# A layer's steps woven between expert picks: other step sizes and choice places, SyncE spreading the picks, states one a step, step sizes taken in the first norm

## The chip, the cores and the metric

The kernel is one program on one core of a Trainium2 chip. The metric is device time in microseconds (us), the median of several runs. PE is TensorE, DVE is VectorE, ACT is ScalarE, POOL is GpSimd, SP is SyncE. All data are 32-bit floats.

## The reference, cut to what matters

Two layers run over 640 tokens: one prompt of 512 tokens and eight streams of 16 tokens. Each layer has two halves:

```
h  = rmsnorm(x, ln1) * (1 + sc1) + sh1            # sh, sc, g come from silu(c) @ w_mod
z, xbc, dt, lx, ly, g_ssd, g_lru = split(h @ w_in)
dt = softplus(dt + bias)                          # the step size of the SSD scan, 16 heads
y_ssd = rmsnorm(ssd_scan(silu(conv(xbc)), dt, states) * silu(z)) @ w_br_ssd
y_lru = (rglru(conv(lx)) * gelu(ly)) @ w_br_lru
x += g1 * ((sigmoid(g_ssd) * y_ssd + sigmoid(g_lru) * y_lru) @ w_out)

h = rmsnorm(x, ln2) * (1 + sc2) + sh2             # the second norm
q = h @ wq                                        # 8 heads, two half keys each
i1, i2 = top16(q1 @ k1.T), top16(q2 @ k2.T)       # 128 keys each
e, g = top16 of the 256 sums, softmax             # 16 experts a head, 128 a token
x += g2 * sum_k gelu(h . u[e_k]) * g_k * v[e_k]   # "picks": rows u, v of 16384 experts
```

The outputs are the normed x, the new scan states of prompt and streams, and the last rows that the convolutions keep.

## The kernel before, in words

**Tiles and regions.** The 640 tokens are five tiles of 128 (the fifth holds the eight streams). The dense work of a layer is done in two regions: tiles 0 to 2 (384 columns) and tiles 3 and 4 (256 columns). That makes regions 0 to 3 over the two layers, and expert tiles 0 to 9. A region is a list of steps, numbered by `bases`: N1 (first norm, 12 steps), X (10 projections with the short convolution), S (the scan: six or so steps a tile), Z, LX, LRU, M (32 projections for the merge), OUT (8 projections, with the second norm's squares and sums among them; the norm itself, from its ninth step on, has no projection), Q (16 projections and the choice of the experts, 22 steps with the last four having no projection). A projection reads one 512 KB tile of weights, which SP loads into one of four slots (`wslot`) as soon as the projection four before it is done. Region 1 and region 3 also carry the stream states: 32 loads of 256 KB in both together, by SP into five slots, and 16 stores by ACT.

**Picks.** A unit is one pick for each of the 128 tokens: POOL gathers 128 rows of 8 KB (u and v of an expert, 1 MB in all) into a ring of eight slots. DVE takes the dot product with h (`dots`), ACT makes gelu, gate and a small diagonal matrix (`diagonals`), PE multiplies with the v half (`values`) and so frees the slot (`used`). Two units are a pair. A tile has 64 pairs, and there are 640 pairs.

**The order of the work.** `plan` writes one list of (pair, steps) entries that every engine follows in program order. `window` deals a region's steps over a given row of pairs by the weights in `SHARE`: region 1 over what is left of tile 0 and tiles 1 and 2, region 2 over tiles 3 and 4 (pairs 9 to 122), region 3 over tiles 5 to 7 (pairs 9 to 180), the final norm over tiles 8 and 9. PE multiplies the pair before it, then does the steps; DVE takes the pair first, then the steps; ACT does the first step, the pair, then the other steps. Region 0 comes before all pairs but the last few steps.

**The choice.** In Q, DVE finds the best keys of all tiles of the region and completes the choice of the region's first tile. The choice of the other tiles (`sum_up`, `look_up`, `put`, 24 pieces in 24 pairs, then the gates) is made beside the pairs of the tile before: from pair `choice_at(s)` on, which is 24 in tile 0 and 8 in the others. Picks and gates then stand by token and have to be turned to units: `spread` does it with 16 small DMAs, issued by ACT at pair `choice_at(s) + 28`, and for a region's first tile at Q's last step (in region 0 in two halves, at Q 13 and 21). The first gather of a tile waits for its spread.

**dt.** `x_stage` of PE does the dt projection at X's first step, ahead of the first X projection: 8 matmuls of 16 columns for each tile, after the last slice of h.

**States.** `stream_parts` in S of regions 1 and 3, from its step 9 on: two states a step, each a matmul on PE, a multiplication and an addition on DVE, and a store by ACT. SP has all 16 state loads of a layer in one row between the loads for Z 3 and Z 4, and the last three of them wait for stores.

Of the kernel before, what the change touches and what calls it, by code (L numbers as in the profile page):

```python
# [34 lines left out]
SLOTS = 4  # L35
# [22 lines left out]
def bases(g):  # L58
# [8 lines left out]
    b["END"] = b["Q"] + 22  # L67
    return b
# [11 lines left out]
SHARE = {"N1": 4, "X": 14, "S": 10, "Z": 18, "LX": 17, "LRU": 25, "M": 17, "OUT": 10, "Q": 24}  # L80
# [83 lines left out]


# [25 lines left out]
def choice_at(s):  # L191

    return 8 if s else 24
# [38 lines left out]
def build(nc, a):  # L232
    ctx = ExitStack()
    with ctx:
# [164 lines left out]
        with nc.Block() as block:  # L399
            @block.sync  # L400
            def _(sp):
# [31 lines left out]
                def states(l):  # L433

                    lay = G[1]
                    for i in range(16):
# [10 lines left out]
                for r in range(REGIONS):  # L447
                    l, g = divmod(r, 2)
                    if g == 0:
                        small_ones(l)  # L450
                    for j in range(10):
                        load(tile(l, TX + j))
                        if r == 0 and j == 3:
                            for c in range(4, 8):
                                mod_chunk(c)
                        if r == 0 and 4 <= j < 8:
                            mod_chunk(4 + j)
                    if r == 0:
                        for c in range(12, 16):
                            mod_chunk(c)  # L460
                    for j in range(8):
                        if g and j == 4:
                            states(l)
                        load(tile(l, TZ + j))
                        if r == 0 and j >= 4:
                            mod_chunk(12 + j)
                    for j in range(8):
                        load(tile(l, TLX + j))
                        if r == 0 and j < 4:
                            mod_chunk(20 + j)  # L470
                    for j in range(8):
                        load(tile(l, TLY + j))
                        load(a["w_gate"].rearrange("l k p c -> p (l k) c")[:, l * KT + j, :], 2 * P)
                    for j in range(8):
                        for first in (TGS, TBS, TGL, TBL):
                            load(tile(l, first + j))
                    for j in range(8):
                        load(tile(l, TOUT + j))
                    for j in range(16):
                        load(tile(l, TWQ + j))  # L480
# [1492 lines left out]
```

## Time and profile before

| | |
|---|---|
| median of 3 runs | 4614.37 us (4608.49 to 4616.39) |
| profiled execution | 4609.44 us |
| its span, first to last instruction | 4607.7 us |
| PE, DVE busy | 3212.4 us (70%), 2825.9 us (61%) |
| ACT, POOL busy | 1466.3 us (32%), 1436.5 us (31%) |
| DMA | 1610.83 MB, mean 350 GB/s |
| first gather | at 709.0 us |
| last gather | at 4572.5 us |

Busy time is what an engine spent in instructions; the share is of the span. The gathers are 1342 of the 1611 MB. The page divides the span into 40 slices of 115 us; one digit or number of a row is one slice.

### The profile page before, as it was taken

To read this page: it belongs to the slowest core of one execution; us is meant where nothing else is said; L and a number is where in the kernel's file an instruction comes from. 1 tells how busy PE (TensorE), PEld (TensorE's weight loads), DVE (VectorE), ACT (ScalarE), POOL (GpSimd) and SP (SyncE) were. 2 spreads that over 40 slices of the span, in tenths; PEclk is the share of its full clock that TensorE was granted. 3 is DMA by queue.
4 is the path that set the end of the run, shared out by engine and by line. 5 is a ranking of instruction groups with operands and counts; after the bars stand their busy time and mean duration, and the time that the engine had idled before them with its cause. 6 is when DMAs were issued, how large, how long until landed. Compare 5 with 4: busy or idle time off the path is not lost. (4 is left out here: it accounts for less than half of the span.)

```text
span 4607.7 us, 60395 instructions
## 1 busy us (share of the span) xinstructions
PE 3212.4 (70%) x21986; PEld 1895.2 (41%) x21986; DVE 2825.9 (61%) x6591; ACT 1466.3 (32%) x4657; POOL 1436.5 (31%) x1298
## 2 busy tenths in 40 slices
PE   7899994777777664488999864767777664444443
PEld 4455552445454442254555431445555442121111
DVE  2422058695864587676743696965854587675454
ACT  2224012443622222333722222433622222232222
POOL 0000003333334334323333323334334334344332
PEclk8999996878888776589999875778888786555555
DMA  7333328899999999968999978999999999999998
GB/s 320 142 147 101 101 82 320 343 356 379 417 417 419 419 400 396 413 265 311 382 380 378 366 292 364 395 364 406 418 418 419 420 404 390 421 420 421 421 422 336
DMA packets 279860, 1610.83 MB, mean 350 GB/s; under 512 B 56410, under 2 KB 61328, under 8 KB 112524
## 3 DMA queue, kind: packets, MB, share of 16 engines
q0 software_dynamic: 184320, 1342.26, 71.6%
q1 hardware_dynamic: 65808, 255.49, 14.5%
q10 hardware_dynamic: 29436, 9.24, 0.8%
q8 instruction: 174, 2.85, 0.2%
q14 instruction: 122, 1.00, 0.1%
HBM read 1597.63 MB, written 7.91 MB: 348 GB/s over the span
## 5 line engine op out<-in xcount | busy, mean ns | idle before, releaser
L528 POOL DMA_INDIRECT ring<-in_peer_uv,units x1280 | 1433.3, 1120 | 3136.3 <-PE psum L923 2219.9
L1827 DVE SCALAR_TENSOR_TENSOR ring<-ring,hrow 128x1024 f32<-128x1024 f32 x1280 | 1538.4, 1222 | 890.7 <-DMA ring<-in_peer_uv,units 864.3
L923 PE MATMUL psum<-ring,diag 128*32 128x256 f32 x10240 | 926.0, 495 | 1182.9 <-ACT diag L1292 1181.9
L541 PE MATMUL psum<-hT,wslot 128*128 128x384 f32 (+1 forms) x4224 | 1283.0, 461 | 27.7 <-DMA wslot<-in_w_tiles 24.6
L541 PEld LDWEIGHTS psum<-hT,wslot 128*128 128x128 f32 x4224 | 845.7, 205 | 456.9 <-issue 111.1
L923 PEld LDWEIGHTS psum<-ring,diag 128*32 128x32 f32 x10240 | 322.2, 131 | 1705.1 <-ACT diag L1292 1394.1
L1282 ACT ACTIVATE gel<-hid 128x2 f32<-128x2 f32 x640 | 129.1, 202 | 1935.5 <-DVE ring L1827 1881.0
L541 PE MATMUL psum<-region,wslot 128*128 128x384 f32 (+1 forms) x1536 | 446.8, 446 | 5.5 <-DVE xT L1682 2.2
L541 PEld LDWEIGHTS psum<-region,wslot 128*128 128x128 f32 x1536 | 293.8, 195 | 152.0 <-issue 28.2
L1292 ACT ACTIVATE diag<-pick,wgt 128x32 f32<-128x32 f32 x1280 | 331.7, 306 | 0.0
L1286 ACT ACTIVATE wgt<-gel,units 128x1 f32<-128x1 f32 x1280 | 307.4, 287 | 20.9
L1449 DVE SCALAR_TENSOR_TENSOR region<-region,vec 128x384 f32<-128x384 f32 (+1 forms) x144 | 80.8, 561 | 145.6 <-ACT region L1056 142.4
L945 PE MATMUL psum<-ident,hT 128*32 128x128 f32 x2816 | 129.6, 343 | 37.8 <-ACT hrow L1322 28.4
L945 PEld LDWEIGHTS psum<-ident,hT 128*32 128x32 f32 x2816 | 108.7, 143 | 71.7 <-issue 26.9
L1194 ACT ACTIVATE region<-psum 128x384 f32<-128x384 f32 (+1 forms) x64 | 27.6, 431 | 315.3 <-PE psum L541 305.3
L1827 DVE DVE_READ_ACCUMULATOR ring<-ring,hrow 128x1 f32 x1280 | 104.1, 81 | 0.0
L1662 DVE SCALAR_TENSOR_TENSOR region<-region,psum 128x384 f32<-128x384 f32 (+1 forms) x32 | 15.5, 485 | 142.7 <-PE psum L541 142.6
L1586 DVE SCALAR_TENSOR_TENSOR region<-region,psum 128x384 f32<-128x384 f32 (+1 forms) x32 | 15.5, 485 | 117.8 <-ACT region L1138 117.8
L1656 DVE SCALAR_TENSOR_TENSOR region<-region,psum 128x384 f32<-128x384 f32 (+1 forms) x32 | 15.5, 485 | 110.8 <-PE psum L541 67.1
L1282 ACT ACT_TABLE_LOAD x60 | 77.0, 1283 | 13.1 <-issue 10.9
L572 PE MATMUL psum<-ring,cT 128*32 128x512 f32 x384 | 47.9, 618 | 30.9 <-DMA ring<-in_w_modt 15.6
L1017 ACT ACTIVATE region<-psum 128x512 f32<-128x512 f32 x24 | 14.3, 597 | 153.6 <-PE psum L580 141.8
(247 smaller groups left out, 2806.0 us busy)
## 6 DMA issues: line engine op xcount, KB each, us to landing
wslot<-in_w_tiles SPq DMA_DIRECT2D x360, 512.0 KB, 7.7
ring<-in_w_modt SPq DMA_DIRECT2D x24, 2048.0 KB, 9.0
ring<-in_peer_uv,units POOLq DMA_INDIRECT x1280, 13.7
wslot<-in_w_gate SPq DMA_DIRECT2D x32, 128.0 KB, 9.6
region<-in_states_t SPq DMA_DIRECT2D x16, 256.0 KB, 13.2
region<-in_states_n SPq DMA_DIRECT2D x16, 256.0 KB, 10.0
out_new_ssd_sample<-region ACTq DMA_DIRECT2D x16, 256.0 KB, 15.4
xT<-in_x_t SPq DMA_DIRECT2D x1, 2560.0 KB, 8.9
```

What stands on the lines that cost most here:

```text
L528: pool.indirect_dma_start(ring[:, n, :], None, table, bass.IndirectOffsetOnAxis(ap=units[:, s % 2, block, 0, quad:quad + 1].bitcast(U32), ...
L541: last = pe.matmul(out, wslot[:, n % SLOTS, k * P:(k + 1) * P], src(k), start=k == 0, stop=k == KT - 1)
L572: last = pe.matmul(bank(5)[32 * q:32 * q + 32, :], cT[:, 2 * q + kk, :], w, start=kk == 0, stop=kk == 1)
L923: last = pe.matmul(psum[c * BLOCK:(c + 1) * BLOCK, block % 2, block // 2 * 256:(block // 2 + 1) * 256], diag[:, n, :], ring[:, n, D + c * ...
L945: last = pe.matmul(out[c * BLOCK:(c + 1) * BLOCK, :], v, ident[:], start=True, stop=True)
L1194: act.activation(lay.gates[:, q, :], bank(3 + 2 * q)[:, 0:lay.N], ACT.Tanh, scale=0.5).then_inc(S["mg"], 1)
L1282: act.activation(gel[:, v], hid[:, v], ACT.Gelu_apprx_tanh).then_inc(E["gelu"], 1)
L1286: act.activation(wgt[:, c:c + 1], gel[:, c:c + 1], ACT.Copy, scale=units[:, s % 2, block, 1, quad + u:quad + u + 1])\
L1292: act.activation(diag[:, pick % RING, :], pick32[:], ACT.Copy, scale=wgt[:, pick % 16:pick % 16 + 1])\
L1449: st(dve.scalar_tensor_tensor(y, x[:, k:k + NY], w(k), y, ALU.mult, ALU.add))
L1586: st(dve.scalar_tensor_tensor(lay.zt, lay.zth[:, j % 2, :], 1.0, bank(3 + j % 2)[:, 0:lay.N], ALU.add, ALU.mult))
L1827: dve.scalar_tensor_tensor(out=ring[:, n, 0:D], in0=ring[:, n, 0:D], scalar=1.0, in1=hrow[:, e % 2, :], op0=ALU.mult, op1=ALU.mult, accum_ ...
```

## The change

Five things change. (1) `SHARE` has two more entries: the norm part of OUT (`N2`) and Q's last four steps (`QE`) get small sizes of their own, OUT's projections a larger one, and S and LRU move by one. (2) The choice beside tiles 0 and 3 starts at pair 30, not 24 and 8. (3) SP issues the spreads instead of ACT, between its weight loads, in the order of the plan. (4) The dt matmuls are dealt over steps 6 to 9 of N1 as the slices of h come; the stream tile's stay at X 0. (5) States go one a step in eight steps, not two a step in four; the last three state loads of a layer stand behind the loads for LX 0, 1 and 2.

```diff
+    b["N2"], b["QE"] = b["OUT"] + 9, b["Q"] + 18
-SHARE = {"N1": 4, "X": 14, "S": 10, "Z": 18, "LX": 17, "LRU": 25, "M": 17, "OUT": 10, "Q": 24}
+SHARE = {"N1": 4, "X": 14, "S": 11, "Z": 18, "LX": 17, "LRU": 24, "M": 17, "OUT": 18, "N2": 3, "Q": 24, "QE": 6}
...
 def choice_at(s):
-    return 8 if s else 24
+    return {0: 30, 3: 30}.get(s, 8)
...
# SP: the loads become a generator, weights(), and the plan is walked
-                        if g and j == 4:
-                            states(l)
+                            if g and j == 4:
+                                states(l, range(13))
...
+                            yield load(tile(l, TLX + j))
+                            if g and j < 3:
+                                states(l, (13 + j,))
...
+                def spread(s, h):
+                    sp.wait_ge(E["ready"], s + h + 1 if s == 0 else s + 2)
+                    if s >= 2:
+                        sp.wait_ge(E["wgt"], (s - 1) * UNITS)
+                    c = slice(h * length(s), (h + 1) * length(s)) if s == 0 else slice(0, QUADS)
+                    for block in range(BLOCKS):
+                        for r in range(BLOCKS):
+                            sp.dma_start(units[...], picked[...]).then_inc(E["spread"], 16)
+                ahead, taken = weights(), 0
+                for e, steps in PLAN:
+                    while n < min(taken + SLOTS, REGIONS * LOADS):
+                        next(ahead)
+                    if e and e[0] < TILES_E and same_group(e[0]) and e[1] == choice_at(e[0]) + 28:
+                        spread(e[0] + 1, 0)
+                    for r, i in steps:
+                        if r < REGIONS:
+                            taken += loads_in(r, i)
+                            if r == 0 and i == BASE[0]["Q"] + 13:
+                                spread(0, 0)
+                            if i == BASE[r]["Q"] + 21:
+                                spread(TILE0[r], passes(TILE0[r]) - 1)
...
# PE, x_stage
+                def steps_of_dt(lay, u, k):
+                    return pe.matmul(bank(7)[:, u * HEADS:(u + 1) * HEADS], hT[:, k, lay.t0 + u * P:lay.t0 + (u + 1) * P],
+                                     wdt[:, k * HEADS:(k + 1) * HEADS], start=k == 0 and u == 0, stop=k == KT - 1, skip_group_check=True)
+                    if -6 <= i < -2:
+                        if i == -6:
+                            pe.wait_ge(S["mean"], at("mean", 2 * r))
+                            pe.wait_ge(loaded["wdt"], 16 * (l + 1))
+                        pe.wait_ge(S["modulated"], at("modulated", 2 * r, 2 * i + 13))
+                        for k in (2 * i + 12, 2 * i + 13):
+                            for u in range(lay.nt - lay.sample):
+                                last = steps_of_dt(lay, u, k)
...
# PE, stream_parts; DVE and ACT alike
-                    if 9 <= i <= 12:
+                    if 9 <= i <= 16:
+                        j = i - 9
-                        for j in (2 * i - 18, 2 * i - 17):
...
# ACT: spread() and its three calls are gone
-                    if r == 0 and i == 13:
-                        spread(0, 0)
-                    if i == 21:
-                        spread(s, passes(s) - 1)
...
-                        if p == choice_at(s) + 28:
-                            spread(s + 1, 0)
```

## Rows read from the trace of the kernel before

**Rows 1.** The page: the span, and GB/s moved in 40 slices.

```profile
span 4607.7 us, 60395 instructions
GB/s 320 142 147 101 101 82 320 343 356 379 417 417 419 419 400 396 413 265 311 382 380 378 366 292 364 395 364 406 418 418 419 420 404 390 421 420 421 421 422 336
```

**Rows 2.** Busy time in stretches (length, engines, PEclk, DMA, GB/s): regions 1, 2, 3; tile 9.

```profile
817.00:1932.00 1115.00, 747.84 (x6035) 486.70 (x6028) 765.00 (x1776) 389.98 (x1335) 420.99 (x371) 0.79 0.98 396
1932.00:2861.00 929.00, 762.99 (x4548) 416.21 (x4546) 613.59 (x1451) 326.26 (x942) 296.10 (x256) 0.88 0.88 342
2861.00:3995.00 1134.00, 759.88 (x5992) 490.20 (x5984) 784.50 (x1808) 396.31 (x1368) 438.72 (x387) 0.79 1.00 405
...
4260.00:4540.00 280.00, 120.61 (x1120) 47.65 (x1120) 143.63 (x242) 70.73 (x296) 108.86 (x112) 0.54 1.01 421
```

**Rows 3.** The page's DMA issues: count, KB each, median us to landing.

```profile
wslot<-in_w_tiles SPq DMA_DIRECT2D x360, 512.0 KB, 7.7
...
ring<-in_peer_uv,units POOLq DMA_INDIRECT x1280, 13.7
...
region<-in_states_t SPq DMA_DIRECT2D x16, 256.0 KB, 13.2
```

**Rows 4.** The spreads: line L1303; timeline about tile 5's; SP's loads.

```profile
L1303 ACTq DMA_DIRECT2D units<-picked x176: 513/612/1439, 696.5 to 4139.0; - x176
...
2780.66 9.74 ACTq L1303 DMA_DIRECT2D units<-picked  x15
...
2792.82 0.94 POOL L528 DMA_INDIRECT ring<-in_peer_uv,units  x1 [7.41 <-PE psum L923]
...
L408 SPq DMA_DIRECT2D wslot<-in_w_tiles x360: 327/328/4229, 6.9 to 3774.4; - x180
```

**Rows 5.** Timeline of PE and POOL (start, us, instruction, idle before): dt of region 0; a gather.

```profile
46.16 10.43 PE L594 MATMUL psum<-wdt,hT 128*128 128x16 f32 x48 [9.30 <-ACT hT L1008]
...
1975.62 0.94 POOL L528 DMA_INDIRECT ring<-in_peer_uv,units  x1 [26.86 <-PE psum L923]
```

**Rows 6.** States: SP's timeline in region 1, and waits of the whole span.

```profile
996.91 57.48 SPq L444 DMA_DIRECT2D region<-in_states_n  x8
...
DVE region L1567 <- DMA region<-in_states_n: 30.7, 4, 12.7
...
PE psum L541 <- DMA wslot<-in_w_tiles: 24.6, 2, 13.2
```

**Rows 7.** Stretches of region 2: X, S, LX, LRU, OUT, N2, Q, QE; last, region 3's N1.

```profile
1955.00:2039.00 84.00, 77.17 (x368) 45.72 (x368) 61.03 (x142) 31.57 (x92) 21.86 (x19) 0.87 0.71 271
2039.00:2126.00 87.00, 65.53 (x523) 35.55 (x523) 81.02 (x141) 38.49 (x85) 23.82 (x18) 0.81 0.65 244
...
2179.00:2236.00 57.00, 55.77 (x344) 30.58 (x344) 41.97 (x72) 24.14 (x74) 17.88 (x16) 1.00 0.92 345
2236.00:2299.00 63.00, 61.38 (x304) 33.32 (x305) 46.93 (x88) 57.34 (x106) 22.53 (x21) 1.00 1.02 414
...
2507.00:2557.00 50.00, 50.00 (x234) 28.36 (x234) 16.70 (x31) 9.68 (x33) 10.01 (x10) 1.00 0.78 298
2557.00:2578.00 21.00, 10.24 (x119) 4.23 (x117) 18.43 (x32) 13.32 (x34) 11.55 (x10) 0.72 0.97 377
2578.00:2750.00 172.00, 133.30 (x788) 75.97 (x788) 145.81 (x542) 42.47 (x144) 50.41 (x47) 0.86 0.89 343
2750.00:2781.00 31.00, 8.22 (x88) 3.78 (x92) 29.03 (x96) 7.23 (x23) 6.58 (x6) 0.50 0.55 206
...
2861.00:2886.00 25.00, 12.93 (x120) 6.58 (x112) 24.35 (x51) 13.51 (x39) 10.93 (x9) 0.70 1.01 420
```

**Rows 8.** Region 2, DVE on the choice's tile `both` alone, in N1, X and S.

```profile
1932.00:1955.00 23.00, 6.78 (x15) 0.71 1.00 404
1955.00:2039.00 84.00, 12.05 (x33) 0.87 0.71 271
2039.00:2126.00 87.00, 16.25 (x40) 0.81 0.65 244
```

More of the change, by code:

```diff
@@ L163, with loads_in @@
 POS = weight_positions()
+LOADS = 98
+TILE0 = [NT * (r // 2) + FIRST[r % 2] for r in range(REGIONS)]
+def loads_in(r, i):
+    return sum(each for name, count, each in (("X", 10, 1), ("Z", 8, 1), ("LX", 8, 1), ("LRU", 8, 2), ("M", 32, 1), ("OUT", 8, 1), ("Q", 16, 1))
+               if 0 <= i - BASE[r][name] < count)
 PER = {"zeroed": 2, "sampled": 2, "modset": 3, "zscaled": 8, "xfill": 18, "conved": 18, "tapped": 18, "kept": 18, "xth": 10, "silued": 10, "acb": 2, "ea": 2, "seg": 4, "e": 4, "w": 2, "y": 2, "ys": 2,
@@ L431, in small_ones, with states @@
                     sp.dma_start(kT[:], a["keys"].rearrange("p (l i k) -> p l i k", l=DEPTH, i=2)[:, l, :, :]).then_inc(loaded["keys"], 16)
-                def states(l):
+                def states(l, loads):
                     lay = G[1]
-                    for i in range(16):
+                    for i in loads:
                         slot = i % 5
@@ new lines, in spread @@
+                def spread(s, h):
[5 more added lines that the diff above has]
+                        for r in range(BLOCKS):
+                            sp.dma_start(units[r * BLOCK:(r + 1) * BLOCK, s % 2, block, :, c],
+                                         picked[block * BLOCK:(block + 1) * BLOCK, s % 2, r, :, c]).then_inc(E["spread"], 16)
@@ L482, in _ @@
+                for _ in ahead:
+                    pass
             @block.gpsimd
@@ L585, in x_stage @@
                     lay = G[g]
+                    if -6 <= i < -2:
[6 more added lines that the diff above has]
+                                last = steps_of_dt(lay, u, k)
+                        if i == -3 and not lay.sample:
+                            last.then_inc(S["dt_mm"], 1)
                     if i == 0:
@@ L589, in x_stage @@
                             pe.wait_ge(S["sampled"], at("sampled", l, 0))
-                        pe.wait_ge(S["mean"], at("mean", 2 * r))
-                        pe.wait_ge(loaded["wdt"], 16 * (l + 1))
-                        for u in range(lay.nt):
                             for k in range(KT):
-                                last = pe.matmul(bank(7)[:, u * HEADS:(u + 1) * HEADS],
-                                                 hT[:, k, lay.t0 + u * P:lay.t0 + (u + 1) * P],
-                                                 wdt[:, k * HEADS:(k + 1) * HEADS], start=k == 0, stop=k == KT - 1)
-                        last.then_inc(S["dt_mm"], 1)
+                                last = steps_of_dt(lay, lay.nt - 1, k)
+                            last.then_inc(S["dt_mm"], 1)
                     if 0 <= i < 10:
@@ L1293, in diagonals @@
                            .then_inc(E["diag"], 1)
-                def spread(s, h):
-                    act.wait_ge(E["ready"], s + h + 1 if s == 0 else s + 2)
-                    if s >= 2:
-                        act.wait_ge(E["wgt"], (s - 1) * UNITS)
-                    c = slice(h * length(s), (h + 1) * length(s)) if s == 0 else slice(0, QUADS)
-                    for block in range(BLOCKS):
-                        for r in range(BLOCKS):
-                            act.dma_start(units[r * BLOCK:(r + 1) * BLOCK, s % 2, block, :, c],
-                                          picked[block * BLOCK:(block + 1) * BLOCK, s % 2, r, :, c]).then_inc(E["spread"], 16)
                 def take_out(o):
```

100 lines of the change are left out of this document (50 added, 50 removed).

## The prediction

> **What bounds the kernel now.** I read the page's slices first, for where the DMA engines are not full, then the busy time of each stretch between the regions' borders, then the waits and landings, and last the timeline at the places where POOL stood longest.
>
> From the seventh slice on the kernel moves gathers, and where nothing else holds it, it moves 417 to 422 GB/s [rows 1]. In tile 9 alone 112 gathers take 280 us, 2.50 us each, at 421 GB/s [rows 2]: a pair costs 5.0 us of DMA and a 512 KB weight tile 1.25 us (0.524 MB over 418 GB/s). Bytes are fixed, so what can be won after the first gather is the time in which the rate is under 418. A stretch loses its length times (1 - rate/418): region 1, 1115 x (1 - 396/418) = 59 us; region 2, 929 x (1 - 342/418) = 169 us; region 3, 1134 x (1 - 405/418) = 35 us [rows 2]. That is 263 us, two thirds of it in region 2, which has 384 columns in every projection and only 113 pairs to hide them. POOL's waits name PE's values, as in [rows 5], but that is only the ring coming free: it says "ring full" in a stretch at 418 GB/s and "late consumers" in one at 300, so I don't price by them.
>
> Within region 2 [rows 7]: X loses 84 x (1 - 271/418) = 30 us (PE 77 of 84 busy at clock 0.87); S loses 36 us (DVE 81 of 87); LX 10; LRU 1; OUT 14 (PE 50 of 50); Q 31 (DVE 146 of 172); QE 16 (DVE 29 of 31). So the path alternates: PE in X, Z to M and OUT, DVE in S, Q and QE.
>
> **The change part by part.** The sum is made against the profiled execution, 4609.4 us, which is 5 us under the median of the three runs.
>
> *dt in the norm's steps.* Region 0 has 24 dt matmuls (48 instructions with the weight loads) in 10.4 us, 0.434 us each, after PE has waited 9.3 us for the last slice of h [rows 5]; region 2 has as many and the same pattern, X 0 stands behind them, and POOL's wait there, 26.9 us, is the longest [rows 5]. Dealt over the slices, two slices are 6 matmuls, 2.6 us. Region 0: the slices come every 0.6 us and the dt work takes 1.3 us a slice, so it starts with the second slice, some 3.5 us before the last: 3.5 us off the serial part ahead of all gathers. Region 2: six slices are out 5 us before the last two there, because a pair and a choice piece stand between, so 7.8 of the 10.4 us go into the wait: 7 us. In regions 1 and 3 one tile of two moves, 8 matmuls = 3.5 us each; these are nearer to DMA-bound, so 4 us for both. Against it: PE now waits in steps 6 to 9 for what ACT does two steps later, with its next values queued behind, so a ring slot may come free a pair's length (5 us) late in three regions; the cover is the ring. I take 15 us, bounds 0 and 28 (10.4 twice and 3.5 twice).
>
> *Spreads from ACT to SP.* 176 issues at 0.612 us hold ACT at each of the 11 spreads, 9.74 us for 15 issues, 10.3 with the first [rows 4]; ACT's diagonals, which PE's values and then the ring wait for, are behind. About tile 5's spread POOL stood 7.4 us [rows 4]. The ring holds four pairs, 20 us of DMA, of which 13.7 are a gather's flight [rows 3], so about 6 us of a 10.3 us block are covered and 4 us are lost where DMA is the bound. The first spread has no pair behind it and gains nothing; tile 5's comes at the last moment (pair 57 of 61) and its gather waits for the landing wherever it is issued, so half of it stays. Ten spreads at up to 4.3 us are 43; tiles 2, 3, 7 and 9 have theirs in full-rate stretches where the row of slices shows no dip [rows 1], so I count six at 3 us: 17 us, bounds 0 and 35. On SP each issue costs between 0.328 us, a weight load's, and ACT's 0.612 [rows 4]: 5 to 10 us in which no weight is loaded, with four tiles loaded ahead, which PE takes in over 20 us (a projection with 384 columns is 5 us, and there is a pair between). No wait of PE, then, beyond the two priced next. A wait is added to SP: the spread waits for the choice, and what stands behind it is the next weight load and, in region 3, the states.
>
> The Trainium skill ("DMA: Bandwidth & Descriptors", section "Issuing engines are not separate DMA queues") says that issuing from another engine saves only the sequencer's issue time, usually small against the transfer. Here the issue time is 10.3 us a spread and the transfer 8 KB, so the row speaks against it; by the rule as written the 17 us would go and the median be 4581 (three quarters of 44), inside the forecast's own range.
>
> *States one a step.* SP sat in the second eight state loads for 57.5 us, and Z 4's weights stood behind [rows 6]: PE waited 24.6 us in all for weights, twice, both there, and DVE 30.7 us for states [rows 6]. With the last three loads put behind LX 0 to 2 and the others not waiting for stores, the 24.6 go; the DVE waits shrink, since a step has one state where it had two. They overlap, and Z's stretches are near DMA-bound, so the 24.6 and 30.7 are worth less than their sum: 19 us for both regions. Against it, in region 3 the spread for tile 6 (pair 36) now stands on SP ahead of the states, where before they were loaded right after Z 3's weights; PE wants the first at pair 38, two pairs or 13 us after the choice is ready, and they come after 5 to 10 us of issues and a landing of 13 [rows 3]: 5 us late, up to 10. I take 14 us, bounds 0 and 30.
>
> *Choice from pair 30.* Beside tile 3 the choice lay wholly in N1, X and S: 6.8, 12.1 and 16.3 us of DVE [rows 8]. Pairs 30 to 53 are S's last two, Z, LX and most of LRU. S was DVE-bound: 81 - 16 + 3 = 68 us of DVE against PE's 66, so 87 becomes about 75: 12 us. N1's chain runs on DVE with the 6.8 us of pieces between: 4 us. X is PE-bound: 4 us. Given back: LX had DVE 42 of 57 and gets 12, LRU 47 of 63 and gets 9 [rows 7], both then almost as full as PE: 3 and 4 us. Net 13 us, bounds -15 (all 35 us reappear, less what S gives) and 30. Beside tile 0 it moves six pairs and I take 2 us. What is late next: the gates are ready at pair 57 and the spread must land before the first gather of the next tile, at pair 61. That is three pairs and more, 18 us in region 1 and 21 in region 2, against 5 to 10 of issues and a landing of 13.7 at most, if it is as slow as a gather's. It fits narrowly; if not, 0 to 5 us each.
>
> *Step sizes.* Worked out from `window`: region 2's S goes from 10 pairs to 11, Z from 7 to 8, OUT from 5 to 8, N2 from 5 to 2, Q and QE together from 27 to 24, M from 29 to 30. OUT and N2 keep 10 pairs together and their time is PE's eight projections plus the norm's chain (50 + 21 us [rows 7]) however they are dealt. Three pairs leave a DVE-bound stretch (3 x 2.4 us) and go where they cost 1.5 to 2.4 each. In regions 1 and 3, N2 gets nine steps in three pairs; region 3's N1 already does twelve in four at 420 GB/s [rows 7], so nothing is lost there. QE's four steps in two pairs put 14 to 17 us of DVE between two dots, against about 14 us of cover: 3 us lost in each region, about what the pairs moved out of Q win. I take 0, bounds -15 and 20.
>
> *Sum.* 15 + 17 + 14 + 13 + 2 + 0 = 61 us. Several of these claim the same lost time (in region 2's first stretches dt and choice, in region 1's Z spread, states and clock), and a stretch that is freed from one holder meets the next; I take three quarters, 46. Then 4609.4 - 46 = 4563, and 4568 for the median.
>
> **The rivals.**
>
> *SP becomes the holder (slower).* If a spread keeps SP from weights for longer than the four slots last, PE stands in M, LX and Q of the regions. Place: the spreads for tiles 1, 2, 4, 6 and 7, and the first loads of regions 1 to 3. It decides from the point where the wait for the choice plus the issues plus a weight's landing (0 + 10 + 8 us) pass four projections with their pairs (25 us). For it: SP is in order, and DVE may be two steps behind PE, which makes the 0 into 10. Against: PE cannot run on without DVE's reads of its banks. Price: 10.3 us of block plus a 2 us late landing at each of eight places, 98 us, against the other parts without the spread's gain (44 x 3/4 = 33): 4609 + 65 = 4674, 4679 as a median.
>
> *Spread queued behind weights.* Spread and weights now share SP's queue. The weights' landing is 7.7 us [rows 3], so a spread issued just behind one lands as much later, and that falls on the first gather of tiles 1, 4 and 5, where there is no slack: 3 x 8 = 24 us. Time 4563 + 24 = 4587, 4592 as a median. For it: tile 5's was tight before; against: when its spread is due the weights of region 3 landed long ago. The Trainium skill (same page, section "Queues, rings and completion order") says that on each DMA engine a queue's descriptors are taken in order while the engine goes round between queues, which is this mechanism.
>
> *Given back.* The ring hides the blocks already, the choice's 35 us reappear in LX and LRU, and only dt's 7 us of regions 0 and 2 and part of the states stay: 4 to 12 us. Time 4605, within what can be told from no change (0.2%, 9 us). For it: PE is at 98% in LX and LRU [rows 7].
>
> *All of it and the evening out.* If S, Q and QE of region 2 (83 us lost) come down by half besides, and the terms hold in full: 61 + 40 = 101, 4508, 4513 as a median. For it: these sizes follow where the rate is low. Against: DVE's own work in Q does not change.
>
> **How the numbers follow.** Forecast 0.66 (4535 to 4600), queued behind weights 0.10, all of it 0.08, given back 0.09, SP the holder 0.07. The forecast's own low end is the upper bounds for two of the terms; its high end a quarter of the sum. The range 4518 to 4614 leaves out most of the fastest case, SP the holder and a little of given back. Faster by over 0.2% are the first three: 0.84. Within 0.2%: 0.09. Slower: 0.07.
>
> **What would show it.** Right: ACT has no DMA of `units` and no 10 us holes in its diagonals; region 2 shortens from 929 to about 900 us, S from 87 to about 75 for a pair more; PE's wait for weights (24.6 us) is gone; X 0 of region 0 starts 3.5 us earlier and the first gather with it. Wrong: a wait of PE for `wslot` of more than 30 us in all (SP the holder); POOL idle for `units` ahead of tiles 1, 4, 5 by over 15 us (behind weights); DVE above 95% busy in LX and LRU with their rates under 330 GB/s (given back). The forecast is wrong if region 2 is not shorter by 15 us.

## The result, and the profile after

The changed kernel takes 4575.1 us (median of four runs, 4572.6 to 4578.7) beside 4611.4 us for the kernel before in the same comparison: a ratio of 0.9923 with a 95% interval of 0.9910 to 0.9935, or 36 us, where the prediction's sum was 46; its 4568 is 7 us under what came. The profiled execution went from 4609.4 to 4574.7 us. The two lines of its page that answer to [rows 1]:

```profile
span 4573.0 us, 60410 instructions
...
GB/s 329 133 152 102 101 79 313 394 375 408 417 418 419 411 416 381 364 340 342 362 366 401 380 275 363 390 377 395 418 418 419 414 415 367 421 420 421 421 421 332
```

The busy time of the three regions, as in [rows 2] (length; busy time of PE, its weight loads, DVE, ACT and POOL; PEclk, DMA share, GB/s), each from the start of its first pair to that of the next region's (region 3 to the final norm's):

```profile
807.00:1902.00 1095.00, 745.32 (x6010) 485.10 (x6008) 763.13 (x1765) 390.28 (x1333) 416.60 (x372) 0.79 1.00 406
1902.00:2814.00 912.00, 767.39 (x4565) 417.66 (x4565) 617.11 (x1461) 333.25 (x950) 302.68 (x257) 0.89 0.90 349
2814.00:3960.00 1146.00, 768.00 (x5988) 496.51 (x5984) 785.04 (x1809) 396.58 (x1368) 446.52 (x387) 0.78 0.99 401
```

With the prediction's own measure, length x (1 - rate/418), called the loss from here on, the regions lose 31, 151 and 47 us, where they were 59, 169 and 35: -28, -18 and +12, in all -34 us. That is the whole difference of the two spans (34.7), so the measure accounts for the change, and the result has three parts: region 1 gained most, region 2 less than was forecast, region 3 lost.

Region 1's X, S, Z and LX in the kernel before, which the rows ahead of the prediction did not show:

```profile
840.00:932.00 92.00, 69.12 (x528) 50.76 (x527) 69.78 (x179) 37.36 (x162) 28.23 (x26) 0.83 0.88 347
932.00:1011.00 79.00, 56.76 (x684) 34.08 (x680) 75.86 (x143) 37.73 (x87) 30.72 (x22) 0.78 0.89 353
1011.00:1089.00 78.00, 55.49 (x414) 36.50 (x406) 43.80 (x85) 21.68 (x76) 22.75 (x21) 0.83 0.96 348
1089.00:1159.00 70.00, 58.79 (x459) 41.95 (x460) 48.03 (x95) 30.77 (x128) 28.26 (x24) 0.86 1.00 403
```

The same four after:

```profile
829.00:919.00 90.00, 65.54 (x562) 45.13 (x561) 65.72 (x156) 38.81 (x167) 34.23 (x31) 0.82 0.98 394
919.00:1000.00 81.00, 61.44 (x732) 37.49 (x728) 78.40 (x150) 38.97 (x92) 33.54 (x24) 0.77 0.93 376
1000.00:1074.00 74.00, 61.77 (x436) 41.04 (x432) 52.52 (x112) 23.75 (x83) 26.59 (x22) 0.86 1.01 382
1074.00:1145.00 71.00, 51.20 (x414) 35.32 (x406) 49.35 (x97) 30.62 (x128) 30.90 (x26) 0.85 1.02 419
```

Every one moves more: the gathers in X (POOL's count) went from 26 to 31 in nearly the same time, and LX is at full rate. N1, ahead of them, went from 339 to 415 GB/s. Region 2's X, S, Z, LX, LRU, OUT and QE after, against [rows 7]:

```profile
1919.00:2003.00 84.00, 79.18 (x400) 47.42 (x400) 52.22 (x106) 35.52 (x99) 21.68 (x20) 0.87 0.76 291
2003.00:2087.00 84.00, 68.01 (x563) 35.68 (x567) 70.90 (x111) 47.98 (x100) 31.77 (x23) 0.83 0.84 315
2087.00:2136.00 49.00, 49.00 (x246) 25.91 (x238) 41.30 (x90) 13.93 (x51) 18.14 (x15) 0.97 0.93 354
2136.00:2201.00 65.00, 61.65 (x360) 33.98 (x360) 52.47 (x106) 25.14 (x76) 22.84 (x18) 0.98 0.93 349
2201.00:2270.00 69.00, 66.17 (x346) 35.69 (x338) 58.06 (x125) 59.15 (x108) 23.76 (x20) 0.97 0.96 372
...
2480.00:2534.00 54.00, 53.81 (x310) 29.98 (x298) 23.26 (x40) 13.49 (x49) 18.95 (x16) 1.00 0.98 403
...
2713.00:2742.00 29.00, 7.95 (x92) 4.62 (x92) 27.02 (x108) 5.69 (x19) 5.62 (x6) 0.62 0.60 229
```

S lost 36 us and loses 21 (DVE 71 of 84 for 11 pairs, where it was 81 of 87 for 10); OUT lost 14 and loses 2, since its projections now carry eight pairs. LRU gave 7 back: it was at 414 GB/s and is at 372. Region 3's S and LX, QE's four steps, and the region's end, from QE's first pair to tile 8's first:

```profile
2933.00:3020.00 87.00, 57.92 (x633) 32.96 (x635) 66.20 (x104) 41.82 (x94) 31.02 (x25) 0.70 0.91 362
3095.00:3178.00 83.00, 53.11 (x397) 35.32 (x400) 51.22 (x101) 30.31 (x129) 30.49 (x26) 0.82 0.98 387
3834.00:3854.00 20.00, 2.06 (x20) 0.72 (x24) 18.80 (x66) 4.98 (x14) 1.87 (x2) 0.50 0.69 287
3834.00:3908.00 74.00, 28.81 (x282) 11.29 (x286) 48.57 (x116) 19.52 (x76) 30.07 (x26) 0.52 0.88 361
```

Here the DMA engines stand partly idle: S loses 12 us with neither PE nor DVE near full, LX and QE lose 6 each. In the kernel before, these three lost 9, 0 and 2. Behind QE's four steps another 4 us go, so the end of the region loses 10, where it lost 5.

Waits of the whole span (us, times, longest), POOL's for picks and PE's for state loads; there is no PE wait for `wslot` any more:

```profile
POOL ring L571 <- DMA units<-picked: 718.9, 3, 703.6
...
PE psum L760 <- DMA region<-in_states_t: 17.8, 8, 7.4
```

And the spread on SP, all 176 issues, then SP's timeline in region 3 around tile 6's spread:

```profile
L505 SPq DMA_DIRECT2D units<-picked x176: 507/591/1523, 695.1 to 4099.2; - x176
...
2975.00 10.15 SPq L505 DMA_DIRECT2D units<-picked  x16
2985.19 20.67 SPq L455 DMA_DIRECT2D region<-in_states_t  x8
```

### The profile page after: what moved, and what is told of

It is laid out like the page before. It is cut to its first block and busy times, and to the rows that moved or that the text cites. A ratio compares the mean times of both kernels' runs of the same rounds, so it can differ in the third digit from the quotient of the medians.

```text
span 4573.0 us, 60410 instructions
## 1 busy us (share of the span) xinstructions
PE 3224.7 (71%) x21986; PEld 1901.7 (42%) x21986; DVE 2828.0 (62%) x6591; ACT 1474.3 (32%) x4662; POOL 1445.4 (32%) x1298
## 5 line engine op out<-in xcount | busy, mean ns | idle before, releaser
L584 PE MATMUL psum<-region,wslot 128*128 128x384 f32 (+1 forms) x1536 | 460.1, 456 | 3.4 <-ACT region L1234 1.9
L584 PEld LDWEIGHTS psum<-region,wslot 128*128 128x128 f32 x1536 | 303.2, 202 | 154.9 <-issue 30.7
L1247 ACT ACTIVATE region<-psum 128x384 f32<-128x384 f32 (+1 forms) x64 | 27.6, 431 | 306.0 <-PE psum L584 305.8
L1282 ACT ACTIVATE region<-psum 128x384 f32<-128x384 f32 (+1 forms) x64 | 27.2, 424 | 120.9 <-PE psum L584 120.7
```

The costliest lines, as they stand in the source:

```text
L584: last = pe.matmul(out, wslot[:, n % SLOTS, k * P:(k + 1) * P], src(k), start=k == 0, stop=k == KT - 1)
L1247: act.activation(lay.gates[:, q, :], bank(3 + 2 * q)[:, 0:lay.N], ACT.Tanh, scale=0.5).then_inc(S["mg"], 1)
L1282: act.activation(lay.qT[:, j % 2, q, :], bank(3 + q)[:, 0:lay.N], ACT.Copy).then_inc(S["q_taken"], 1)
```

## The experiments

All twelve were timed in five rounds against the kernel before on the same chip; the difference from the changed kernel is that of the ratios times 4610 us. A ratio is known to about 0.0014, a difference of two to 0.002 or 9 us. What is smaller than that stays open, unless the traces tell it. Each kernel has one trace, and that has noise of its own: in five of the kernels (the changed one, two states a step, five loads first, state stores on SP, and the last of the table) region 2 has the same program, and it took 912, 906, 900, 908 and 900 us. So a difference of under 12 us in region 2 is no effect of an edit by itself.

| kernel | median us | ratio (95%) | against the changed kernel |
|---|---|---|---|
| spreads on ACT again | 4618.0 | 1.0016 (1.0007 to 1.0025) | +43 |
| choice at 24 and 8 again | 4590.0 | 0.9956 (0.9943 to 0.9970) | +15 |
| only tile 3's choice at 8 | 4577.6 | 0.9934 (0.9921 to 0.9947) | +5 |
| old step sizes | 4570.9 | 0.9927 (0.9913 to 0.9940) | +2 |
| dt at X 0 again | 4580.9 | 0.9938 (0.9925 to 0.9952) | +7 |
| two states a step, loads in a row | 4569.0 | 0.9913 (0.9899 to 0.9926) | -5 |
| spreads on ACT and old choice | 4610.6 | 1.0001 (0.9990 to 1.0011) | +36 |
| before + spreads on SP + new choice | 4589.0 | 0.9956 (0.9943 to 0.9969) | +15 |
| five state loads first | 4565.3 | 0.9908 (0.9895 to 0.9921) | -7 |
| that + state stores on SP | 4575.0 | 0.9927 (0.9912 to 0.9942) | +2 |
| that + no `QE`, tile 0 at 28 | 4584.7 | 0.9949 (0.9936 to 0.9962) | +12 |
| five loads first, two states a step | 4555.6 | 0.9885 (0.9869 to 0.9902) | -18 |

### Each part undone alone

The five kernels are the changed one with one part as it was.

**Spreads on ACT.**

```diff
-                            sp.dma_start(units[...], picked[...])   # SP, in the plan
+                            act.dma_start(units[...], picked[...])  # ACT, at its three old places
```

> The changed kernel with the spreads issued by ACT again, at their old places in ACT's program; all else as changed. Theory A (each of the five parts gives what was priced, times three quarters): 13 us slower than the changed kernel, 4588 us where the changed one is at 4575, ratio to before 0.995; ACT shows 10 us holes of issues, and tile 1's and tile 4's first gathers wait for units as before or longer. Theory B (one lever: the ring hides the 10 us blocks, and the gain comes from step sizes and the choice): under 4 us slower, 4575 to 4579. Theory C (SP's spreads do harm, because the states of region 3 stand behind tile 6's): equal or faster, since PE's 24 us of waits for states in region 3 go.

It is the most expensive part to undo, +43 us: slower than the kernel before, and far from all three theories. ACT's and POOL's timelines in region 1 (start, length, instruction, idle before) show the largest piece:

```profile
1069.81 11.61 ACTq L1159 DMA_DIRECT2D out_new_ssd_sample<-region  x1
...
1089.55 25.49 ACTq L1338 DMA_DIRECT2D units<-picked  x16
```

```profile
1119.85 1.22 POOL L553 DMA_INDIRECT ring<-in_peer_uv,units  x1 [22.98 <-PE psum L958]
```

With the choice at pair 30 the picks of tile 1 come ready just behind ACT's state stores, in ACT's order. The 16 issues don't take 10.3 us there as in [rows 4] but 25.5, ACT's diagonals stand behind them, PE behind the diagonals and POOL behind PE. The stretch, LX of region 1, runs 85 us at 334 GB/s where it is 71 at 419 with SP issuing them; and M of region 2, where tile 4's spread falls, 221 us at 358 against 210 at 378:

```profile
1086.00:1171.00 85.00, 52.57 (x398) 35.54 (x402) 48.71 (x97) 31.20 (x132) 28.65 (x25) 0.80 0.86 334
2295.00:2516.00 221.00, 208.13 (x1086) 112.21 (x1088) 89.42 (x160) 54.81 (x192) 70.97 (x58) 0.96 0.91 358
```

These two are 17 and 12 us of loss. Some 20 more lie at the ends of the regions, each with the spread for the region's first tile (3, 5 and 8), a block of the usual 10 to 11 us on ACT. The row below is region 3's end in this kernel, from QE's first pair on; it loses 15 us where the changed one loses 10. The ends of regions 1 and 2 lose 9 and 29 against 4 and 24, and N1 of region 1, just behind region 0's last spread, 5 against 0:

```profile
3879.00:3959.00 80.00, 26.58 (x284) 10.60 (x288) 48.51 (x116) 19.39 (x76) 30.02 (x27) 0.56 0.83 338
```

**Choice.**

```diff
-    return {0: 30, 3: 30}.get(s, 8)
+    return 8 if s else 24
```

> The changed kernel with the choice at pair 24 of tile 0 and pair 8 of tile 3 again. Theory A: 11 us slower, 4586 us, ratio 0.9945; DVE over 90% busy in region 2's S, whose loss goes back from 21 to over 30 us, while LX and LRU of region 2, which lost 18 us, lose about 10. Theory B: 15 us or more slower. Theory D (the later choice only moves the loss, and tile 1's first gather, which waits 9.4 us for its picks, costs as much as it wins): within 4 us of the changed kernel; the 9.4 us wait of POOL for units is gone.

+15 us. S of region 2 and X of region 1 in this kernel:

```profile
2021.00:2113.00 92.00, 68.05 (x552) 36.39 (x552) 82.61 (x143) 46.97 (x96) 33.14 (x22) 0.83 0.71 268
830.00:927.00 97.00, 71.67 (x560) 48.54 (x552) 75.22 (x187) 38.34 (x167) 31.93 (x31) 0.78 0.94 372
```

Region 2's S takes 92 us for 11 pairs, 8 more, but Z and LRU get 3 and 5 us of it back and the region as a whole loses 153 us against 151. Region 1 loses 45 against 31. Six of these 14 are X's, which has 75 us of DVE instead of 66 and takes 97 us for the same 14 pairs. Six are LX's, in which one state store's issue holds ACT for 16.4 us. By this trace most of it is tile 0's move.

**Only tile 3's choice.**

```diff
-    return {0: 30, 3: 30}.get(s, 8)
+    return {0: 30}.get(s, 8)
```

> The changed kernel with only tile 3's choice at pair 8 again; tile 0's stays at 30. With both back it was 15 us slower. Theory A, as priced: 11 of the 15 are tile 3's, so 4586. Theory I, from the stages of that run (region 1 lost 13 us more, region 2 only 4, since what S loses LX and LRU win): 3 to 5 us slower than the changed kernel, 4579.

This puts the last paragraph to the proof. Region 1 keeps most of its gain (35 us lost against 31); region 2's S is slow again (the row below), and region 2 loses 146 us, not more than the changed kernel's 151. By the traces the place of tile 3's choice moves the loss about and does not take it away. By the times this part is worth 5 us, give or take 9, and tile 0's the other 10, with the same error.

```profile
2007.00:2098.00 91.00, 70.14 (x552) 36.29 (x553) 82.38 (x143) 46.97 (x96) 33.49 (x22) 0.81 0.71 269
```

**Step sizes.**

```diff
-SHARE = {"N1": 4, "X": 14, "S": 11, "Z": 18, "LX": 17, "LRU": 24, "M": 17, "OUT": 18, "N2": 3, "Q": 24, "QE": 6}
+SHARE = {"N1": 4, "X": 14, "S": 10, "Z": 18, "LX": 17, "LRU": 25, "M": 17, "OUT": 10, "Q": 24}
```

> The changed kernel with the old table of step sizes. Theory A: equal to the changed kernel within 4 us, 4571 to 4579: region 2's OUT loses its 12 us again (299 GB/s), but the holes that QE's four packed steps leave (bins of 92 and 8 GB/s at the ends of regions 1 and 3) are gone, 5 us in region 1 and 9 in region 3. Theory B: 15 us or more slower, the sizes are what shortened region 2.

Not to be told from the changed kernel. Underneath, large amounts cancel: OUT of region 2 loses 15 us again (first row below, five pairs in 51 us), while LRU there comes back to 403 GB/s (5 us) and LX of region 3 to 417 (6 us). The ends of the regions gain most. Region 3's, from QE's first pair on (second row), loses 2 us where it lost 10, region 2's 16 where it lost 24, and region 1's nothing where it lost 4. So QE's small size costs 20 us, 18 of them behind its four steps.

```profile
2462.00:2513.00 51.00, 51.00 (x240) 28.91 (x238) 17.70 (x33) 9.82 (x34) 10.56 (x10) 1.00 0.80 298
...
3806.00:3900.00 94.00, 40.66 (x382) 15.23 (x386) 60.31 (x136) 26.55 (x107) 39.87 (x38) 0.54 1.00 409
```

**dt.**

```diff
-                    if -6 <= i < -2:            # PE, N1's steps 6 to 9
+                    if i == 0:                  # PE, all dt ahead of X 0
```

> The changed kernel with the dt matmuls at X 0 again. Theory A: 11 us slower, 4586 us: first gather 2 to 4 us later, region 2's X longer by 7, region 1's and 3's by 2 to 4. Theory B: only the first gather's 2 to 4 us, 4579 at most, the rest is ring slack.

+7 us, inside the timing's error, and between the two theories. PE's and POOL's timelines in region 2, of this kernel and then of the changed one:

```profile
1933.65 10.42 PE L637 MATMUL psum<-wdt,hT 128*128 128x16 f32 x48 [8.52 <-ACT hT L1051]
...
1951.68 0.94 POOL L571 DMA_INDIRECT ring<-in_peer_uv,units  x1 [24.18 <-PE psum L966]
```

```profile
1919.65 7.83 PE L628 MATMUL psum<-wdt,hT 128*128 128x16 f32 x36 [4.82 <-ACT hT L1061]
1930.99 2.74 PE L628 MATMUL psum<-wdt,hT 128*128 128x16 f32 x12
...
1928.80 0.94 POOL L571 DMA_INDIRECT ring<-in_peer_uv,units  x1 [11.92 <-PE psum L976]
1942.81 0.94 POOL L571 DMA_INDIRECT ring<-in_peer_uv,units  x1 [11.83 <-PE psum L976]
```

The long wait of [rows 5] is there again when dt is at X 0, and with dt dealt out it is two waits of 12 us: as long together. X of region 2 takes 84 us in both. X of region 1 takes 92 us against 89, but it also takes 92 to 93 in three kernels in which dt is dealt out and nothing else of that stretch is edited, so this is no sign of dt. What is left is the first gather, 711.5 us against 707.5. That one can be read over all kernels of the study: with dt dealt out it starts at 704.7 to 708.4, and where dt is at X 0 at 709.0, 709.0 and 711.5, so about 3 us are the edit's.

**States.**

```diff
-                    if 9 <= i <= 16:            # PE; DVE and ACT alike: one state
-                        j = i - 9
+                    if 9 <= i <= 12:
+                        for j in (2 * i - 18, 2 * i - 17):
...
# SP
-                                states(l, range(13))
+                                states(l, range(16))
-                            if g and j < 3:
-                                states(l, (13 + j,))
```

> The changed kernel with two states a step in four steps and all 16 state loads between the loads for Z 3 and Z 4. Theory A (each part gives about what was priced): 10 us slower than the changed kernel, 4585 us, ratio 0.9945; PE waits over 20 us for wslot again, in Z of regions 1 and 3. Theory B (those waits lie beside a full ring): within 4 us of the changed kernel, though the waits are back.

-5 us: inside the timing's error, but if the 14 us priced for this part were right, it would be 14 us slower. Neither theory's waits came: of the kernel before's 24.6 us wait for weights [rows 6] 3.8 us are back, once, so it was not the order of the state loads alone that made it. What made it stays open. What one state a step cost is seen in ACT's 16 state stores (least/median/most ns of one issue), in the kernel before, the changed one, and this one:

```profile
L1124 ACTq DMA_DIRECT2D out_new_ssd_sample<-region x16: 378/1230/10720, 1023.9 to 3109.8; - x16
```

```profile
L1177 ACTq DMA_DIRECT2D out_new_ssd_sample<-region x16: 378/379/16959, 1013.0 to 3107.6; - x16
```

```profile
L1175 ACTq DMA_DIRECT2D out_new_ssd_sample<-region x16: 378/596/13488, 1015.0 to 3070.7; - x16
```

Added up, ACT is held 46 us, 71 us and 38 us by these sixteen issues. Over the study it is 38 to 48 us in the four kernels with two states a step, and 68 to 96 in the eight with one where ACT issues the stores. In the changed kernel the last two stand in LX of region 3 (ACT's timeline), and LX loses 6 us that this kernel doesn't lose (75 us at 419 GB/s):

```profile
3094.02 9.14 ACTq L1177 DMA_DIRECT2D out_new_ssd_sample<-region  x1
...
3107.64 15.44 ACTq L1177 DMA_DIRECT2D out_new_ssd_sample<-region  x1
```

### Two parts at a time

**Spreads on ACT and the old choice**: dt, states and sizes alone on top of the kernel before.

> The changed kernel with the spreads on ACT and the choice at pairs 24 and 8 again, both at once. With spreads on ACT alone it was 43 us slower than the changed kernel, with the old choice alone 15. Theory E (the spread on SP is worth its 43 us mainly because the later choice puts tile 1's spread among the state stores on ACT, 25 us of one block, and tile 4's in front of tile 4's first gather): under 4615, about 4605, so that on ACT the old places are better than the new ones by 13 us. Theory F (SP's issue is worth 43 us wherever the choice is): 4615 to 4635.

1.0001: these three parts by themselves give nothing. With the kernel that has the old choice (0.9956) this makes a ladder: nothing for the three, 21 us for moving the spreads to SP, 15 for the choice. And the spreads' place is worth 21 us with the old choice and 43 with the new one: the two edits need each other. The traces say where the 21 lie: in N1 of region 1 and the ends of regions 1 to 3, the same four stretches as above, which lose 22 us less with the spreads on SP. They also say why the three parts give nothing here: the three ends lose 54 us in this kernel and 25 in the kernel before, and this eats what OUT and the others win. The packed steps of QE and a 10 us block of ACT stand close together there.

**Before, with the spreads on SP and the new choice only.**

> The kernel before with two of the five parts alone: spreads on SP, and the choice from pair 30 in tiles 0 and 3. Old step sizes, dt at X 0, states two a step. Theory J (these two carry the whole gain; the kernel with the other three parts and not these two was level with the one before, 4610.6 against 4610.3): 4570 to 4578, ratio 0.992. Theory A (the five add up as priced): 4590.

0.9956, so 20 us for the two alone, as the sum of the parts had it and not the theory that they carry the whole gain. The three parts that were worth 0 without them are worth 15 on top. Region 2 loses 157 us here against 151 (OUT 15 against 2), region 1 41 against 31 (Z 12 against 6). PE's wait for weights is 0.7 us here, with the old order of the state loads. Whether the three parts need the spreads on SP, or the new choice, or both, no run separates fully: with the spreads on SP and the old choice the kernel is at 0.9956, but SP's spreads alone were not timed.

### Versions meant to be better

**Five state loads first.** The prediction had 5 to 10 us against the states in region 3, because tile 6's spread stands ahead of them on SP. The first five are put ahead of Z 3's weights, and so of the spread.

```diff
+                            if g and j == 3:
+                                states(l, range(5))
                             if g and j == 4:
-                                states(l, range(13))
+                                states(l, range(5, 13))
```

> The changed kernel with the first five state loads of a layer moved one weight load ahead, before Z 3's, so that in region 3 they stand on SP ahead of tile 6's spread instead of behind it. Theory G (that order costs region 3 its loss: PE waited 24 us for states in S there and 13 holes of a few us follow): 5 to 9 us faster than the changed kernel, 4568, region 3's loss 43 to about 35 us and PE's waits for states_t under 10 us. Theory H (the ring covers PE's wait): within 3 us.

S of region 3 for the same 14 pairs, 78 us where it was 87:

```profile
2926.00:3004.00 78.00, 56.02 (x631) 31.33 (x634) 65.82 (x103) 41.36 (x94) 33.71 (x24) 0.76 0.99 397
```

PE's waits for the transposed states go from 17.8 to 10.7 us. So the price named in the prediction was real, and at its high end. The median is 7 to 10 us lower, about the error of the timing; the profiled execution is 15.6 us shorter, but 12 of those lie in region 2, where nothing was edited: see the last section.

**State stores on SP besides**, since ACT's issues of them hold the diagonals.

```diff
-                            act.wait_ge(S["sadded"], at("sadded", l, j))
-                            act.dma_start(dst[:, l, j, :, :], lay.states[...])
+                    sp.wait_ge(S["sadded"], at("sadded", l, j))
+                    sp.dma_start(dst[:, l, j, :, :], G[1].states[...])
```

> The kernel with the first five state loads moved ahead (4565), and besides the 16 state stores issued by SP at the same places of the plan instead of by ACT. On ACT the 16 issues took 76 us in that kernel, 0.38 us each where the queue is short and 7 to 17 us where two stores are still under way. Theory K (such an issue holds its engine until the queue drains, as the spread did behind them for 25 us, and ACT's holes in Z and LX starve the ring): 6 to 12 us faster, 4555; ACT's holes gone. Theory L (SP held for 10 to 16 us at a time now starves PE of weights in Z and LX instead): equal or slower, with PE waiting over 20 us for wslot.

It loses what the five loads had gained. The issues hold SP for less in all, 30 us against ACT's 76, but one of them takes 16.94 us (SP's timeline), and behind it on SP stand state loads and weights (DVE's and PE's waits):

```profile
1033.86 16.94 SPq L515 DMA_DIRECT2D out_new_ssd_sample<-region  x1
```

```profile
DVE region L1609 <- DMA region<-in_states_n: 48.7, 2, 24.6
...
PE psum L595 <- DMA wslot<-in_w_tiles: 12.0, 2, 9.6
```

In its time this is theory L, though PE's wait for weights is 12 us and not over 20. It is the rival of the prediction in which SP becomes the holder, at a small scale: what decides is not which engine issues a transfer but what stands behind it there while it is held.

**No `QE` size, and tile 0's choice at 28**, on top of that.

```diff
-SHARE = {... "Q": 24, "QE": 6}
+SHARE = {... "Q": 24}
...
-    return {0: 30, 3: 30}.get(s, 8)
+    return {0: 28, 3: 30}.get(s, 8)
```

> The kernel of st_sp with, besides, no small size for Q's last four steps (24 like the rest of Q) and tile 0's choice from pair 28. Theory M: the holes at the ends of regions 1 and 3 (6 and 9 us: bins of 92 and of 8 and 59 GB/s) go, and POOL's 9 us wait for tile 1's picks; 5 to 12 us faster than st_sp. Theory N (what the pairs win at the end of Q they lose in front of it, and tile 0's later choice was worth the wait): within 4 us.

10 us worse than without the two, which neither theory had. The ends of the three regions do get 19 us back, as with the old sizes. But the pairs that stand there now are missing elsewhere: region 2 loses 154 us instead of 146 (Q 36 against 30, LX and LRU 23 together against 18), LX of region 1 11 instead of 7, Z of region 3 12 instead of 9. A size moves the pairs of every other stretch with it. Which of the two edits costs the 10 us was not tested.

**Five loads first and two states a step.**

```diff
+                            if g and j == 3:
+                                states(l, range(5))
                             if g and j == 4:
-                                states(l, range(13))
+                                states(l, range(5, 16))
...
# no state loads behind LX 0 to 2; PE, DVE and ACT take two states a step, as in the run of that part
```

> The changed kernel, with the state loads of regions 1 and 3 in another order: in region 3 the first five are issued ahead of Z 3's weights (and so ahead of tile 6's spread), the other eleven in a row behind Z 4's, and the states taken two a step again, as before the change. The two edits alone gave 4565.3 (first five ahead, against 4575.1) and 4569.0 (two a step). Theory A (independent: the first takes away the wait of a late load at the start of region 3's S, the second shortens ACT's blocked store issues): 4575 - 10 - 6 = 4559, within 3. Theory B (both get back the same wait of PE for the states in region 3's S): 4565, within 3. Theory C (the eleven loads in a row, ahead of Z 5's weights with no spread between, keep SP from weights again, as the 57.5 us row of the kernel before): 4572 or more, with a PE wait for wslot over 10 us.

0.9885: the best kernel of the study, 18 us faster than the changed one, and the independent sum (theory A, 4559) holds. Region 3's S and LX have both gains, 78 us at 400 GB/s and 75 at 419:

```profile
2923.00:3001.00 78.00, 56.95 (x630) 31.73 (x633) 65.83 (x102) 41.68 (x94) 32.97 (x24) 0.76 0.99 400
3081.00:3156.00 75.00, 52.80 (x417) 35.85 (x415) 50.30 (x98) 31.03 (x131) 31.01 (x26) 0.88 1.02 419
```

PE waits 8.2 us for weights again, so theory C has a little of the truth: Z of region 3 loses 8 us instead of 6.

## Why the prediction was right, and where its sizes were not

The forecast was 4568 in 4535 to 4600, and 4575 came. The way was the one described: the gathers' rate rose where it had been low. But single terms were off by more than the whole was, and that the sum came out is in part luck. The steps one by one:

- *Spreads to SP*, priced 17 us (0 to 35), with three quarters taken of all: measured 21 us with the old choice and 43 with the new. Mis-sized, and the largest error. The term was built on the row of a spread that is not held, 0.61 us an issue. That an issue on ACT can be held was in the trace of before, where two of the state stores take over 10 us each; it was not looked at. That the new choice would move tile 1's picks right behind those stores, 25.5 us for 16, was not seen. And the spread for tile 3 was counted as free, because the kernel before has full rate there; behind QE's small size it costs 5 us. The Trainium skill ("DMA: Bandwidth & Descriptors", section "Issuing engines are not separate DMA queues") says that what a second issuing engine saves is usually small against the transfer. Here it was worth 21 to 43 us: the 16 issues of a spread, 8 KB each, take 10 to 11 us of an engine's time, and how long the transfers themselves take no row shows.
- *Choice*, priced 13 for tile 3 and 2 for tile 0: measured 15 ± 9 together, and by the traces the other way round. The prediction wrote that of tile 3's 35 us some 7 reappear; S is 8 us shorter than with the old choice, for the same 11 pairs, and Z, LX and LRU gave nearly all of it back, as in the rival "given back", though DVE has only 52 of 65 and 58 of 69 us in LX and LRU. Tile 0's six pairs were dismissed in half a sentence; they take 10 us of DVE out of a stretch of region 1 in which DVE and PE alternate.
- *States*, priced 14 (0 to 30): measured -5 ± 9, so mis-sized and perhaps of the other sign. Two of its pieces came: the 24.6 us wait for weights is gone, and region 3's states stand behind tile 6's spread, which costs 9 us. But all except 3.8 us of the wait for weights stays away with the old loads, and dealing the states out makes ACT's stores hold it for longer, 71 us instead of 46, which no step of the prediction looked at: of a step that is dealt out, the stores go with it.
- *dt*, priced 15 (0 to 28): 7 ± 9 measured, of which the traces show 3. Region 2's 7 us were none: the wait of 26.9 us was split into two of 12. PE is busy 79 of 84 us of X there, and to do its work in other places leaves its amount, which fits but was not tested by itself. The 3.5 us of region 0 were nearly there: X 0's first matmul comes at 53.7 us instead of 56.4, and the first gather about 3 us earlier over all fourteen kernels.
- *Step sizes*, priced 0 (-15 to 20): measured 2 ± 9. Right in sum and not in its pieces. OUT wins 12 us, which the prediction put at nothing, since OUT and N2 keep their pairs together. The ends of the three regions lose 4, 8 and 8 us, where 3 each were priced. LX and LRU get pairs they can't hide.
- *Sum.* The three quarters were meant for parts that claim the same loss. The ladder shows something stronger: three parts are worth 0 or 15 us, by whether the other two are there. So a sum with a common factor was right in size by compensation, which is luck: spread too low, states and dt too high.

Of the marks: no transfer of `units` on ACT, yes; PE's wait for weights gone, yes; region 2 shorter by 17 us, at the edge of the 15 asked and not the 29 forecast, and the same program of region 2 took 4 to 12 us less in other kernels' traces; S 84 us and not 75, each for a pair more. Against the rivals: DVE is 81% and 84% busy in LX and LRU, not 95; SP never was the holder. POOL did wait for `units` ahead of tiles 1 and 5 (9.4 and 6.0 us, in all 15.4), which is just over the 15 us that were the mark of "queued behind weights"; but LX of region 1, in which 9.4 of these lie, moves 419 GB/s, so the ring covered that one, and the median is 17 us under that rival's.

## What to carry to other kernels

An issue of a transfer isn't free for the engine that makes it, and its price was not constant here: 10 us or 25 for the same 16 issues. Before moving one, list what is queued ahead of it and what the engine must do behind it, at the new time and not at the old. Where several engines take turns as the bound, measure edits in pairs: here three edits gave nothing alone and 15 us on top of two others. And when pairs are moved out of a stretch, follow it up to the next one that runs at full rate: of the 20 us that QE's size cost, 18 lay behind its own steps.

## What the runs showed of the hardware

**The issue of a store can hold its engine for many times its usual length.** The issue of a 256 KB state store takes 0.38 us at best. In the changed kernel six of the sixteen take 6 to 17 us on ACT (16.96 at most); on SP it was one of sixteen (16.94). The spread behind such stores took 25.5 us for 16 issues where 10.3 is usual. Having earlier stores under way is not enough for it: in the kernel before an issue took 10.43 us at 1039.8 with two stores not yet landed, and another 0.38 us at 1055.2, also with two. What fills up, and at what amount, was not measured.

**TensorE's granted clock differs between profiled executions where the instructions are the same.** Region 2's X, S and Z in the kernel with five state loads first, whose region 2 has no edit:

```profile
1923.00:2003.00 80.00, 75.47 (x400) 45.23 (x400) 51.93 (x105) 35.27 (x99) 21.73 (x20) 0.92 0.79 302
2003.00:2083.00 80.00, 64.24 (x567) 33.75 (x567) 71.00 (x111) 48.00 (x101) 33.28 (x23) 0.87 0.84 333
2083.00:2131.00 48.00, 48.00 (x244) 25.69 (x237) 41.71 (x90) 14.60 (x54) 18.46 (x15) 1.00 0.94 363
```

The same matmuls take 188 us here at a granted 0.92, 0.87 and 1.00 and 196 in the changed kernel at 0.87, 0.83 and 0.97, and the three stretches are 208 and 217 us long. The clock has two levels, 1.2 and 2.4 GHz, and these shares say how long each was granted. What sets off the lower one here wasn't tested, nor whether it goes with the kernel or with the execution; it stays open, and it means that one profile's difference of up to 12 us in region 2 isn't by itself an effect of an edit.
